# A down projection as Strassen products over five blocks, accumulated in SBUF, in a decoder-step kernel

## What is computed

```
h2 = modulate(rms_norm(x, lw['ln2_g']), sh2, sc2)
ff = (jax.nn.silu(h2 @ lw['w_gate']) * (h2 @ lw['w_up'])) @ lw['w_down']
x = x + g2[:, None, :] * ff
```

## Time and profile before

| | before |
|---|---|
| median of 3 runs | 1400.41 us (1399.22 to 1403.49) |
| the profiled execution | 1400.21 us, its span 1398.6 us |
| TensorE busy | 1314.4 us, 94% |
| VectorE, ScalarE, GpSimd busy | 63%, 44%, 43% |
| mean granted TensorE clock | 0.967 of full |

### The profile page before, as it was taken

The page is one execution under the profiler, slowest core; times in us unless marked ns, Lnnn a source line. Parts: engine busy times, 40 slices in busy tenths (PEclk is TensorE's granted clock), DMA queues, the critical chain, the costliest instruction groups (busy, mean ns, idle before and its releaser), DMA issues.

```text
span 1398.6 us, 24565 instructions
## 1 busy us (share of the span) xinstructions
PE 1314.4 (94%) x9185; PEld 1187.3 (85%) x9185; DVE 874.7 (63%) x1791; ACT 618.8 (44%) x1069; POOL 596.5 (43%) x418
## 2 busy tenths in 40 slices
PE   6889999989579999899999999999999999999998
PEld 4566998887446555699999999999999999999997
DVE  6757889866779844767993344444334466666664
ACT  5536888825967764445533333333333321010002
POOL 0332549992000000255477677767766732121210
PEclk9899999999699998999999999999999999999999
DMA  9622115432101114275412333312332174242203
GB/s 354 235 66 65 47 57 165 157 121 76 31 16 31 52 52 143 75 241 178 126 61 92 106 107 122 111 72 92 122 121 92 61 303 181 92 182 99 114 0 122
DMA packets 117799, 158.65 MB, mean 113 GB/s; under 512 B 16071, under 2 KB 99343, under 8 KB 114608
## 3 DMA queue, kind: packets, MB, share of 16 engines
q1 hardware_dynamic: 117680, 157.08, 32.5%
HBM read 123.99 MB, written 33.10 MB: 112 GB/s over the span
## 4 chain that ended last, share of the span: by engine, by line
PE 69%; DVE 7%; ACT 5%; SPq 5%; POOLq 4%; issue 3%; POOL 3%; DVEq 3%; ACTq 1%; DMA 0%
PE ps L2941 29%; PE ps L2967 6%; PE ps L2966 6%; PE ps L2968 6%; PE ps L2698 2%; PE ps L2686 2%; PE ps L2805 2%; PE ps L2807 2%; PE ps L2806 2%; SPq L600 2%; PE ps L2676 1%; SPq L599 1%; ACT junk L1142 1%; DVEq L2242 1%; POOLq L930 1%
## 5 line engine op out<-in xcount | busy, mean ns | idle before, releaser
L870 POOL TENSOR_TENSOR wL<-wraw,wH 128x1024 fp32r<-128x1024 f32 x36 | 88.5, 2463 | 296.0 <-ACT wH L1135 294.6
L1557 DVE SCALAR_TENSOR_TENSOR xh<-ps,mod,xh 128x344 f32<-128x344 f32 (+1 forms) x264 | 150.3, 571 | 60.4 <-PE ps L2968 60.4
L2941 PE MATMUL ps<-comb,opH 128*128 128x258 f32 x960 | 155.4, 284 | 2.6 <-DVE af L2230 2.6
L2941 PEld LDWEIGHTS ps<-comb,opH 128*128 128x128 f32 x960 | 133.3, 191 | 2.8 <-POOL opL L988 2.8
L988 POOL TENSOR_TENSOR opL<-wsum,opH 128x512 fp32r<-128x512 f32 x80 | 110.2, 1381 | 48.7 <-ACT opH L1436 45.4
L1436 ACT CAST opH<-wsum 128x512 fp32r<-128x512 f32 x80 | 49.6, 622 | 181.3 <-PE ps L2941 98.5
L2941 PE MATMUL ps<-h2H,opL 128*128 128x258 f32 x640 | 129.1, 283 | 0.0
L2941 PE MATMUL ps<-h2L,opH 128*128 128x258 f32 x640 | 129.1, 283 | 0.0
L2941 PE MATMUL ps<-h2H,opH 128*128 128x258 f32 x640 | 128.8, 283 | 0.0
L993 POOL TENSOR_TENSOR dL<-draw,dH 128x1024 fp32r<-128x1024 f32 x22 | 52.5, 2404 | 169.7 <-ACT dH L1507 169.7
L1142 ACT ACTIVATE junk<-score,keyX 128x896 bf16<-128x896 f32 (+2 forms) x96 | 106.0, 1106 | 18.7 <-DVE keyX L1809 13.9
(11 more groups left out here) (484 smaller groups left out, 3851.7 us busy)
## 6 DMA issues: line engine op xcount, KB each, us to landing
adb<-in_ada_w SPq DMA_DIRECT2D x8, 2048.0 KB, 8.3
wraw<-in_w_out SPq DMA_DIRECT2D x24, 512.0 KB, 4.6
draw<-in_w_down SPq DMA_DIRECT2D x22, 512.0 KB, 9.1
raw<-in_w_gate SPq DMA_DIRECT2D x10, 1024.0 KB, 8.5
raw<-in_w_up SPq DMA_DIRECT2D x10, 1024.0 KB, 5.0
ffn_products<-a_odd SPq DMA_DIRECT2D x4, 2064.0 KB, 7.8
ffn_products<-a_even SPq DMA_DIRECT2D x4, 2064.0 KB, 7.4
a_third<-ffn_products SPq DMA_DIRECT2D x3, 2064.0 KB, 8.0
```

What stands on the lines that cost most here:

```text
L870: pool.tensor_tensor(wL[s][:], wraw[s][:], wH[s][:].bitcast(F32), ALU.subtract).then_inc(s_wL, 1)
L1557: return V.scalar_tensor_tensor(out=out, in0=in0, scalar=scalar, in1=in1, op0=op0, op1=op1)
L2941: ins = mm(ps[:, sum_bank(v, p) + h, 0:HC], weight[s][:, k, :], token[:, k, h * HC:(h + 1) * HC], start=begins, stop=ends, skip_group_chec ...
```

## The change

Pairs 1 to 10 of the down projection are taken as five blocks (`NBLK`) of two pairs. In each block the two pairs are the halves of the inner width, the 1024 output columns are cut in halves of 512, the tokens in halves of 516, and seven products (order `DOWN_P` = 1, 6, 7, 5, 2, 4, 3) take the place of eight. A product is 4 groups of 12 matmuls of 258 columns, each group in two banks. Seven accumulators `acc1` to `acc7` in SBUF (128 x 2064 each) hold the sums over the five blocks: ScalarE copies the first block's products out of PSUM, VectorE adds those of the others. Pair 0 is done last, in the plain form with 24 groups.

The seven token operands of a block are now made in the feed-forward stage: `input_sum` (four subtractions of 1032 columns, VectorE), `input_high` (ScalarE), `input_low` (VectorE), and SP stores each of the seven to DRAM. Of the fifth block six are made and stored while the first block's products run. GpSimd makes four weight sums a block (`down_sum`) from a 2 MB load and 7 low parts of 1024 columns. Seven closing sums join the accumulators: three by VectorE in the last block, four by GpSimd. VectorE then adds four results of 4 x 516 columns to the residual, among the last 24 groups. The residual is loaded after product 6.

```diff
+DOWN_P = (1, 6, 7, 5, 2, 4, 3)
+ND = 7 * NBLK
+INPUTS = (1, 5, 2, 3, 6, 7, 4)
...
+            for d in range(ND):
+                if d == 7:
+                    all_stored(in_queue(NBLK - 1, 4) + 1)
+                    for hf in range(2):
+                        sp.dma_start(xh[hf][:], spill[:, KH * hf:KH * (hf + 1), :]).then_inc(s_xr[hf], 16)
+                    for f in range(2):
+                        sp.dma_start(lasta[f][:].bitcast(F32), a_spill[:, f]).then_inc(s_la[f], 16)
+                if d + A_SLOTS < ND:
+                    load_input(d + A_SLOTS)
+                if d < 6:
+                    store_input(NBLK - 1, (5, 2, 3, 6, 7, 4)[d])
+                if d % 7 == 2:
+                    if d // 7 + 1 < NBLK:
+                        load_block(d // 7 + 1)
...
-            for w in range(2 * FB):
-                pool.wait_ge(s_wH, units(len(ITEMS) + w + 1))
-                d = w % DOWN_SLOTS
-                pool.tensor_tensor(dL[d][:], draw[d][:], dH[d][:].bitcast(F32), ALU.subtract).then_inc(s_wL, 1)
+            for b in range(NBLK):
+                pool.wait_ge(s_dr[0], loaded(b + 1))
+                down_sum(5, a21, a22, ALU.add)
+                down_sum(6, dsum[5][:], a11, ALU.subtract)
+                down_low(7 * b)
+                down_low(7 * b + 1)
+                if b == 0:
+                    pool.wait_ge(s_un, units(item(NST - 1, 4) + 1))
+                down_sum(7, a11, a21, ALU.subtract)
+                down_low(7 * b + 2)
+                down_low(7 * b + 3)
+                down_sum(3, a12, dsum[6][:], ALU.subtract)
+                for i in range(4, 7):
+                    down_low(7 * b + i)
+            for w in range(2):
+                down_low(ND + w)
...
+            def joined(x, y):
+                pool.tensor_tensor(acc[x][:], acc[x][:], acc[y][:], ALU.add)
+                pool.drain().then_inc(s_ws, 1)
+
+            pool.wait_ge(s_tc, after(4 + 4 * NBLK + 2))
+            joined(5, 7)
+            pool.wait_ge(s_dne, NG2 - 2 * KH)
+            joined(2, 1)
+            pool.wait_ge(s_dne, NG2 - KH)
+            joined(4, 7)
+            pool.wait_ge(s_dne, NG2)
+            joined(3, 6)
...
+            def first_block_out(d, m):
+
+                act.wait_ge(s_dn, KH * d + m + 1)
+                nc.scalar.copy(two(acc[DOWN_P[d]][:, m, :]), ps[:, 2 * m:2 * m + 2, 0:HC]).then_inc(s_dne, 1)
+
+            down_high(0)
+            down_high(1)
+            for d in range(7):
+                first_block_out(d, 0)
+                first_block_out(d, 1)
+                if d == 0:
+                    down_high(2)
+                first_block_out(d, 2)
+                first_block_out(d, 3)
+                if d == 0:
+                    down_high(3)
+                down_high(d + 4)
+                if d < 6:
+                    input_high(NBLK - 1, (5, 2, 3, 6, 7, 4)[d])
...
+            def input_sum(b, p):
+
+                x, y = {5: (5, 1), 6: (3, 5), 7: (6, 1), 4: (2, 6)}[p]
+                dve.drain()
+                V.tensor_tensor(down_input(b, p), down_input(b, x), down_input(b, y), ALU.subtract).then_inc(s_tc, 1)
...
+            dve.wait_ge(s_dne, KH * 7)
+            for d in range(7, ND):
+                i = d - 7 * (NBLK - 1)
+                for m in range(KH):
+                    down_add(d, m)
+                    if (i, m) == (2, 1):
+                        joined(6, 1)
+                    elif (i, m) == (3, 1):
+                        joined(7, 6)
+                        dve.drain().then_inc(s_tc, 1)
+                    elif (i, m) == (4, 1):
+                        joined(6, 5)
+                        dve.drain().then_inc(s_tc, 1)
+                    elif (i, m) == (5, 3):
+                        for hf in range(2):
+                            dve.wait_ge(s_xr[hf], loaded(1))
+                        joined_ready(1)
+                        into_x(5, 0)
+                        into_x(5, 1)
+                    elif (i, m) == (6, 0):
+                        into_x(5, 2)
+                        into_x(5, 3)
...
+            joined_ready(2)
+            for m in range(KH):
+                into_x(2, m)
+            dve.drain()
+            for q in range(24):
+                if q == KH:
+                    dve.drain()
+                last_add(q)
+                if q < KH:
+                    if q == 0:
+                        joined_ready(3)
+                    into_x(4, q)
+                elif q < 2 * KH:
+                    if q == KH:
+                        joined_ready(4)
+                        samples_added(3, 0)
+                    into_x(3, q - KH)
...
+            def down_group(d, m):
+
+                grp = KH * d + m
+                if grp >= 4:
+                    pe.wait_ge(s_dne, grp - 3)
...
+                pe.wait_ge(s_dne, NG2 - 3 + q // 2 if q < 8 else NG2 + (q - 5 if q < 14 else q - 1))
```

More of the change, by code:

```diff
@@ L350, in build @@
         s3 = at("s3", [P, HW], RP + 24768)
-        sgf = at("sgf", [P, 2, NTOK], RP + 16512)
-        A_AT = {"first": T4_AT, "even": A_X, "odd": A_X + 16512, "third": RH + 36864, "fourth": T4_AT}
-        aR = {n: at(f"a_{n}", [P, 2, 2, NTOK], off, F32R) for n, off in A_AT.items()}
-        D_RAW = (RING, RING + 4096, RING + 24576, Q5)
-        D_HL = (RING + 8192, RING + 16384, RING + 28672, Q5 + 4096)
-        draw = [at(f"draw{i}", [P, KD, P], D_RAW[i]) for i in range(DOWN_SLOTS)]
-        dH = [at(f"dH{i}", [P, KD, P], D_HL[i], F32R) for i in range(DOWN_SLOTS)]
@@ L366, in summed @@
+        b_spill = nc.dram_tensor("down_inputs", (NBLK, 7, P, 2, 2, HW), F32).ap()
         def summed(v, p):
@@ L1540, in _, with down_high @@
-            for w in range(2, 2 * FB):
-                down_high(w)
+            def down_high(d):
+                p = DOWN_P[d % 7]
+                if d >= ND:
+                    act.wait_ge(s_dr[1 + d - ND], loaded(1))
+                elif p in (1, 2, 4):
+                    act.wait_ge(s_dr[0], loaded(d // 7 + 1))
+                else:
+                    act.wait_ge(s_ws, after(2 * NST + 4 * (d // 7) + (5, 6, 7, 3).index(p) + 1))
+                if d == 0:
+                    act.wait_ge(s_wL, units(item(NST - 2, 4) + 1))
+                elif d == 1:
+                    act.wait_ge(s_wL, units(len(ITEMS)))
+                elif d < 4:
+                    act.wait_ge(s_un, units(len(ITEMS) - (3 if d == 2 else 1)))
+                else:
+                    act.wait_ge(s_dn, KH * (d - 3))
+                w = down_weight(p) if d < ND else lastw[d - ND][:]
+                nc.scalar.copy(dO[d % DOWN_OPS][0][:], w).then_inc(s_wH, 1)
@@ L1543, in _ @@
+            for d in range(11, ND + 2):
+                down_high(d)
             for i in range(ALLT):
@@ L2342, in _ @@
                     block21(v)
[L2343 to L2351 removed]
+            input_low(NBLK - 1, 5)
+            input_low(NBLK - 1, 2)
+            input_low(NBLK - 1, 3)
+            for p in (6, 7, 4):
+                input_sum(NBLK - 1, p)
+                input_low(NBLK - 1, p)
@@ new lines, in down_add, with joined, joined_ready @@
+            def down_add(d, m):
+                p = DOWN_P[d % 7]
+                dve.wait_ge(s_dn, KH * d + m + 1)
+                V.tensor_tensor(two(acc[p][:, m, :]), ps[:, 2 * m:2 * m + 2, 0:HC], two(acc[p][:, m, :]), ALU.add
+                                ).then_inc(s_dne, 1)
+            def joined(x, y):
+                dve.drain()
+                V.tensor_tensor(acc[x][:], acc[x][:], acc[y][:], ALU.add)
+            def joined_ready(n):
+                dve.wait_ge(s_ws, after(2 * NST + 4 * NBLK + n))
@@ L2352, in down_add, with last_add @@
+            def last_add(q):
+                n, c = q % KD, q // KD
                 w = CW if c < 2 else TAIL
-                bank = 6 + q % 2 if last else q % 8
-                dve.wait_ge(s_dn, 24 * i + q + 1)
+                dve.wait_ge(s_dn, NG2 + q + 1)
                 xp = xh[n // KH][:, n % KH, c * CW:c * CW + w]
+                bank = last_bank(q)
                 if c == 2:
```

370 lines of the change are left out of this document (213 added, 157 removed).

## The result

| | before | after |
|---|---|---|
| median of 4 runs each, same chip | 1401.79 us (1399.22 to 1403.49) | 1416.42 us (1414.05 to 1419.32) |
| the profiled execution, its span | 1400.21, 1398.6 us | 1415.01, 1413.2 us |
| TensorE busy | 1314.4 us, 94% | 1295.0 us, 92% |
| mean granted TensorE clock | 0.967 | 0.958 |

What follows compares the result with a forecast made beforehand. TensorE, busy for 94% of the span, was taken as the bound. The terms -24.8 + 1.5 + 13.4 + 9.2 + 8.7 + 10.3 - 0.8 + 0.3 gave +17.8 us, hence 1418.0 us, range 1403 to 1427.

Steps and rivals of the forecast that it cites:

- Matmuls, -24.8 us: Down projection: 1680 matmuls of 258 columns and 144 of 344 replace 1584 of 344, 24.8 us less if nothing waits.
- The feed-forward stage, nothing: Feed-forward stage: VectorE's and GpSimd's added work fits beside TensorE's, so no time is lost.
- rival E: Feed-forward stage loses its cover, 1 to 1.5 us in each of four blocks: 1423 us; chance 0.08.
- The start, +1.5: Start of the down projection: GpSimd's first weights ready at 15.8, feed-forward ends at 14.4; TensorE waits 1.5 us.
- The first block, 7.4 + 5.2 + 0.75: First seven products: ScalarE's copies queue behind weight waits; 7.4 us before product 5, 5.2 before 7, 0.75 in small pieces.
- The reload, +9.2: Behind the first block: input 10 queues behind residual and first pair's products, so TensorE waits 9.2 us.
- the three terms: The terms that hang on the transfer queue; at about 358 GB/s they would grow by about 8 us, to 1426.
- Ahead of the last groups, 8.5 + 0.2: End of the products: VectorE's additions to x wait behind GpSimd's sums, freeing banks late; TensorE loses 8.5 and 0.2 us.
- Among the last groups, 10.3 + 0.3: Last 24 groups: VectorE's additions to x hold TensorE 10.3 us, 6.6 at group 8; 0.3 more at the transposes.
- B: Rival: VectorE and GpSimd do not exclude each other in this work; 1395.5 us, faster by 0.35%; chance 0.08.
- C: Rival: queue serves later transfers beside earlier ones, or weights come as fast as alone; 1404 us; chance 0.09.
- D: Rival: stores and loads together run slower, at 380 GB/s, adding 5.3 us: 1423 us; chance 0.12.

Runs made afterwards that it cites:

- e6: Changed kernel with ScalarE's copies of products 4, 5 and 6 ahead of weight high parts, and the reload spread over products 12 to 21: 1396.4 us.
- e2: Changed kernel with the residual's halves loaded at products 12 and 14 and the first pair's products at 19 and 21: 1406.4 us.
- e8: Changed kernel with GpSimd's four closing sums left out, their quarters added into x unsummed: 1408.6 us.
- e3: Changed kernel with each of GpSimd's four closing sums made as four instructions of 516 columns: 1417.4 us.
- e4: Changed kernel with all seven closing sums on VectorE, none on GpSimd: 1415.0 us.
- e10: Changed kernel with ScalarE's copies first, later reload, second weight block ahead of the store, last additions into x later; GpSimd keeps its four sums: 1394.7 us.
- e1: Changed kernel with ScalarE's weight high parts of products 7, 8 and 9 made after the copies of products 4, 5 and 6: 1407.5 us.

## Why the prediction was right, and where its terms were off

**Matmuls, -24.8 us.** Held; the rate between the waits was the one taken from the feed-forward stage. In e6 the 28 products behind the last wait take 161.9 us, 5.78 each for 5.76.

**The feed-forward stage, nothing.** Held, rival E is out. From 740 to 1120 TensorE is busy for all of 380.00 us, with 3166 matmuls for 3167 before, though VectorE and GpSimd do 30 and 34 us more there. After:

```profile
740.00:1120.00 380.00, 380.00 (x3166) 380.00 (x3166) 184.67 (x177) 138.94 (x220) 308.23 (x208) 1.00 0.36 132
```

**The start, +1.5.** 1.40, for GpSimd's first low part, as put.

**The first block, 7.4 + 5.2 + 0.75.** The waits are 7.70 and 2.73 us. ScalarE's timeline shows the first as it was told: the high part of the landed block stands ahead of an input's high part and the copies.

```profile
1156.92 0.59 ACT L1655 COPY acc<-ps 128x516 f32<-128x516 f32 x1 [0.85 <-PE ps L3183]
1167.70 1.04 ACT L1650 CAST down_H<-down_block 128x1024 fp32r<-128x1024 f32 x1 [10.19 <-DMA down_block<-in_w_down]
1168.65 1.05 ACT L1570 CAST staged<-gf 128x1032 fp32r<-128x1032 f32 x1
1169.61 2.05 ACT L1655 COPY acc<-ps 128x516 f32<-128x516 f32 x4
...
1183.72 1.04 ACT L1650 CAST down_H<-dsum 128x1024 fp32r<-128x1024 f32 x1 [5.27 <-POOLq L1063]
```

The second is smaller by 2.5 us, in part since TensorE came to it later: products 5 and 6 took 13.3 us for 11.5, at less than full clock. That is the term that the prediction lacked. Of the 0.75 us in small pieces no wait shows.

**The clock after a wait: not in the prediction.** Its sum took every matmul at the full granted clock. In the changed kernel the clock fell to 0.50, which is 1.2 GHz, during each of the long waits, and TensorE's first matmuls behind it were sent at that level, for 3.2 to 3.7 us:

```profile
1162.00:1168.00 6.00, 0.63 (x6) 0.42 (x4) 0.00 (x0) 0.30 (x1) 0.16 (x1) 0.91 1.02 403
1168.00:1174.00 6.00, 3.67 (x18) 3.70 (x19) 4.17 (x2) 3.99 (x7) 5.57 (x3) 0.53 0.43 168
1174.00:1180.00 6.00, 6.00 (x52) 6.00 (x52) 4.78 (x3) 3.81 (x6) 6.00 (x2) 1.00 0.85 308
1206.00:1213.00 7.00, 0.00 (x0) 0.00 (x0) 0.15 (x1) 0.55 (x1) 2.34 (x1) 0.63 1.01 426
1213.00:1217.00 4.00, 2.68 (x12) 2.71 (x13) 0.00 (x0) 0.00 (x0) 0.00 (x0) 0.50 1.02 427
```

What it costs is read off the products. After: 227.0 - 201.8 of matmuls - 19.3 of waits (7.70, 2.73, 8.90) = 5.9 us. In e6, where waits of 2.51 and 0.66 us are left and the clock stays at 1.00 all through, 206.0 - 201.8 - 3.2 = 1.0 us. So some 5 us of the 21.2 us that e6 gained were clock, and a wait of 8.9 us was worth 10.1 (e2). A clock of 0.50 is also seen behind the waits of 2.73 and 4.00 us (1188 to 1190, 1382 to 1384). Behind a short wait it can go either way: it stays at 1.00 behind the 2.51 us of e6, and falls behind the 2.49 us before the transposes in e8 (that matmul starts at 1380.19):

```profile
1378.00:1381.00 3.00, 0.81 (x7) 0.82 (x8) 2.92 (x6) 0.12 (x1) 0.00 (x0) 1.00 0.00 0
1381.00:1385.00 4.00, 4.00 (x18) 4.00 (x17) 2.35 (x5) 0.95 (x2) 0.00 (x0) 0.57 0.32 131
```

So the length of the wait alone does not decide, and what does the runs don't settle.

**The reload, +9.2.** 8.90, with some luck. (The prediction's own times, 95.9 and 86.9, give 9.0.) Counted from the first down matmul, the reload was issued at 59.6 us for 60.9 put, input 10 landed 21.2 us behind that for 19.1, and TensorE came to it at 71.9 for 71.0. From 1190 to 1220 the queue moved 406, 412 and 420 GB/s in stretches of 10 us; 431 were taken. The Trainium skill's 358 GB/s ("SBUF — State Buffer", the summary of rules for kernel authors), by which the prediction had the sum at 1426, is below what this trace shows; the measurement decides. Redone with that figure of the Trainium skill, as an estimate, the 12.7 MB that the three terms name take 6 us longer than at 431 GB/s, where the prediction has about 8.

**Ahead of the last groups, 8.5 + 0.2.** 7.72. GpSimd's sum of 2064 columns took 4.60 to 4.75 us, 4.67 were estimated. (The prediction has the two VectorE instructions of the earlier trace rows ending with GpSimd's; by the rows they end 0.55 us behind it, and that they waited for it still follows.) Two additions into x stood behind two such sums, 10.07 us together, and the addition that frees the banks behind them:

```profile
1357.43 10.07 DVE L1688 SCALAR_TENSOR_TENSOR xh<-acc,mod,xh 128x508 f32<-128x508 f32 x2 [1.91 <-POOLq L1086]
1367.42 0.68 DVE L2508 TENSOR_TENSOR acc<-ps,acc 128x516 f32<-128x516 f32 x1
...
1371.42 7.17 DVE L1688 SCALAR_TENSOR_TENSOR xh<-acc,mod,xh 128x516 f32<-128x516 f32 x4
```

**Among the last groups, 10.3 + 0.3.** They took 40.7 us for 31.8, so 8.9; as waits 4.00 us at group 8 for 6.6, 1.36 before the transposes for 3.0. VectorE was at the addition in question 1.7 us sooner than put. And TensorE was slower to come there: eight groups took 9.3 us from 1368.25 on, for 7.6 at full clock. Where VectorE ends a stretch, as here, TensorE's slower clock only takes from its wait and costs nothing.

**The sum.** By pieces: start 1.4 for 1.5; products 227.0 for 224.4 (201.8 + 13.4 + 9.2), 2.6 more; wait 7.7 for 8.7; last groups 8.9 for 10.6. Together 17.6 for 17.8 us over the kernel before, from the end of the feed-forward stage to the last copy. So part of the closeness is luck: an unforeseen 5 to 6 us of clock stood against 2.5 + 0.75 us too much in the first block and 2.7 us too much at the end. What lies outside this stretch was taken as before. In the profiled executions the part ahead of it was 1.4 us shorter and the tail behind the last copy 1.6 us: 1400.2 + 17.6 - 1.4 - 1.6 = 1414.8, for 1415.0 measured; the median is 1416.4.

**Rivals.** B (no exclusion) is refuted by the additions of 5.17 us, and e3, e4, e8 and e10 take the lock away piece by piece. C is refuted by the landings in order, by the wait of 8.90 us and by e2, which takes it away. D was right in one thing: with stores and loads in the queue there were stretches at 281 to 289 GB/s, and the block took 12.3 us to land for 10.1 put. But it was issued 21.9 us behind the first matmul for 39.3 - 15.9 = 23.4, so it landed at 34.2 for 33.5: two errors that nearly cancel. The forecast's statement that the copies stand behind ScalarE's high part, and the one on the reload, are shown by e1 and e2, and e6 shows that the two are independent.

## What to carry to other kernels

Fewer matmuls are worth their time only where the operands come as fast as TensorE uses them and the banks are emptied as fast as it fills them: here 24.8 us of saving met 34 us of waits and 5 us of slower clock, and 21 us of that (e6, with its share of the clock) were nothing but the order of two lists, ScalarE's and SP's. On an engine whose list is in program order, put what frees a bank ahead of what waits for a transfer. Before work with two SBUF inputs goes to GpSimd "beside" VectorE, look what VectorE does at that time: four sums cost 12.4 us there and 7.9 us on VectorE itself, though GpSimd had nothing else to do.

## What the hardware showed that I had not expected

- A wait of TensorE can cost more than itself: the granted clock was 0.50 at the end of waits of 7.7 and 8.9 us and for 3.2 to 3.7 us of matmuls behind them; the reload's 8.9 us were worth 10.1 us, ScalarE's 7.7 + 2.7 us became 2.55 + 0.66 and were worth 10.3 us.
- A queue at a busy share of 0.90 to 0.93 moved 281 to 289 GB/s in a stretch with an input's store and an input's load, and 406 to 420 in the stretches of the reload. Shortly after, a store and a load moved at 400 and more, so stores alone are not the reason; the share of busy time does not give the rate.
- A part of the program that no edit touched differed by 6.4 us between executions of kernels that are the same there (1133.5 to 1139.9 us). An edit worth 3 to 5 us had to be read from a stretch of the trace, and not from the median.
